# Multiplying the expert one-hots by their gates on ScalarE instead of VectorE

## The reference, cut to what matters

```python
def peer_ffn(h, wq, subkeys, u_tab, v_tab):
    ...
    eidx = jnp.take_along_axis(cidx, pos, axis=-1)    # i1 * 128 + i2
    gate = jax.nn.softmax(best, axis=-1).astype(h.dtype)
    ...
    def expert_block(args):
        hx, ex, gx = args
        act = jax.nn.gelu(jnp.einsum('td,tkd->tk', hx, u_tab[ex]))
        return jnp.einsum('tk,tkd->td', act * gx, v_tab[ex])
```

## Time and profile before

| | us |
|---|---|
| median of 3 runs | 3662.87 |
| lowest and highest | 3655.67, 3663.2 |
| span of the profiled execution | 3655.0 |

### The profile page before, as it was taken

One profiled execution on the slowest core, in us unless ns is written; L12 is line 12 of the kernel. 1 busy time (PEld: TensorE's weight loads), 2 busy tenths in 40 slices (PEclk: granted clock), 3 DMA queues, 4 the chain that ended last, 5 costly groups with the idle time before them and its releaser, 6 DMA issues. The chain is left out here.

```text
span 3655.0 us, 46514 instructions
## 1 busy us (share of the span) xinstructions
PE 3308.5 (91%) x18811; PEld 2594.7 (71%) x18811; DVE 2606.1 (71%) x3318; ACT 1266.7 (35%) x1467; POOL 414.2 (11%) x393
## 2 busy tenths in 40 slices
PE   7989878989889998999999979898999998999898
PEld 5756646788889998778777768666874674543676
DVE  5856768889999997678788854746446444894664
ACT  3323233334445554444444343312322111100333
POOL 0011101100121221133232100011000110000000
PEclk8889889999999999999999989999999999999899
DMA  9974367847989999899999765223645215442663
GB/s 358 379 274 139 115 224 285 314 167 251 330 322 353 363 362 362 322 371 382 369 376 379 274 205 195 80 76 108 216 162 190 67 31 147 138 154 94 220 222 150
DMA packets 294613, 870.30 MB, mean 238 GB/s; under 512 B 33584, under 2 KB 108436, under 8 KB 242432
## 3 DMA queue, kind: packets, MB, share of 16 engines
q1 hardware_dynamic: 257616, 670.64, 51.7%
q0 software_dynamic: 34320, 190.40, 13.6%
q10 hardware_dynamic: 2464, 6.29, 0.5%
HBM read 820.22 MB, written 46.38 MB: 237 GB/s over the span
## 5 line engine op out<-in xcount | busy, mean ns | idle before, releaser
L2489 DVE TENSOR_TENSOR expert_w_low<-expert_w,expert_w_high 128x2048 fp32r<-128x2048 f32 x256 | 585.5, 2287 | 151.1 <-ACT expert_w_high L2916 148.7
L2824 PE MATMUL bank<-h_halves,expert_w_high 128*128 128x384 f32 x2048 | 610.4, 369 | 61.7 <-DVE expert_w_low L2489 61.5
L2916 ACT ACTIVATE expert_w_high<-expert_w 128x2048 fp32r<-128x2048 f32 x256 | 490.4, 1916 | 443.7 <-DMA expert_w<-in_peer_v_dram 298.8
L294 DVE TENSOR_TENSOR weights_low<-weights,weights_high 128x1024 fp32r<-128x1024 f32 (+4 forms) x288 | 338.2, 1177 | 297.4 <-ACT weights_high L277 294.0
L2825 PE MATMUL bank<-h_halves,expert_w_low 128*128 128x192 f32 x2048 | 519.7, 254 | 0.0
L277 ACT ACTIVATE weights_high<-weights 128x1024 fp32r<-128x1024 f32 (+4 forms) x288 | 293.6, 1022 | 468.3 <-PE bank L322 385.2
L2824 PEld LDWEIGHTS bank<-h_halves,expert_w_high 128*128 128x128 f32 x2048 | 393.3, 192 | 72.5 <-DVE expert_w_low L2489 72.1
L2825 PEld LDWEIGHTS bank<-h_halves,expert_w_low 128*128 128x128 f32 x2048 | 399.6, 195 | 0.0
L2893 PE MATMUL bank<-expert_w_high,gated_acts_halves 128*128 128x512 f32 x512 | 203.0, 396 | 22.4 <-DVE expert_w_low L2489 22.1
L2895 PE MATMUL bank<-expert_w_high,gated_acts_halves 128*128 128x512 f32 x512 | 201.0, 393 | 0.0
L2894 PE MATMUL bank<-expert_w_low,gated_acts_halves 128*128 128x512 f32 x512 | 200.9, 392 | 0.0
(11 more groups left out here) (741 smaller groups left out, 6460.5 us busy)
## 6 DMA issues: line engine op xcount, KB each, us to landing
expert_w<-in_peer_u_dram SPq DMA_DIRECT2D x128, 1024.0 KB
expert_w<-in_peer_v_dram SPq DMA_DIRECT2D x128, 1024.0 KB
weights<-in_ada_w_dram SPq DMA_DIRECT2D x88, 512.0 KB, 9.2
weights<-in_w_out_dram SPq DMA_DIRECT2D x32, 1024.0 KB, 13.3
weights<-in_w_in_dram SPq DMA_DIRECT2D x32, 960.0 KB, 8.7
weights<-in_w_in_dram SPq DMA_DIRECT2D x32, 928.0 KB, 9.8
weights<-in_w_in_dram SPq DMA_DIRECT2D x56, 512.0 KB, 7.3
s_gates_w<-in_w_in_dram SPq DMA_DIRECT2D x56, 512.0 KB, 3.5
```

The lines of the kernel that those rows point to most:

```text
L294: dve.tensor_tensor(self.low[:, u % self.UNITS_HELD, :, 0:n], self.buf[b][:, k:k + self.UNIT, 0:n], self.high[:, u % self.UNITS_HELD, :, 0 ...
L2489: dve.tensor_tensor(wl[:, n % RING, :], w_sb[:, n % RING, :], wh[:, n % RING, :], ALU.subtract).then_inc(wl_ready, 1)
L2824: pe.matmul(o[:, 0:2 * DENSE], uh[:, b, k, :], acts.both[:, k, :, 0:DENSE], start=(k == 0), stop=False)
L2916: act.activation(wh[:, n % RING, :], w_sb[:, n % RING, :], ACT.Copy).then_inc(wh_ready, 1)
```

## The change

The in-place multiplication of `hot1` leaves VectorE's program, and with it the two waits of VectorE for itself; the one-hot now signals `first_onehots_ready`. In ScalarE's program the first tile of each group gets, behind `high` and the gelu, a wait for that signal and eight activations of the kind Copy, one for each token, in place on 128 columns, with the token's column of `gateT` as the scale of each partition. The last of them signals `first_onehots_gated`, for which TensorE now waits, beside `hot_ready`, ahead of the gates products of the group. What is computed stays the same.

```diff
--- before.py
+++ after.py
@@ -2473,6 +2473,7 @@
         sk_loaded, turned = m.sem("subkeys_loaded"), m.sem("peer_q_turned")
         shifted, expd, ready, turned_picks = m.sem("best_shifted"), m.sem("best_exp"), m.sem("picks_ready"), m.sem("picks_turned")
         hot_ready, hot_used = m.sem("onehots_ready"), m.sem("onehots_used")
+        first_hot_ready, first_hot_gated = m.sem("first_onehots_ready"), m.sem("first_onehots_gated")
         gates_ready, gates_stored = m.sem("block_gates_ready"), m.sem("block_gates_stored")
         score_ring = BankRing(m.banks[4:8], m.sem("score_banks_filled"), m.sem("score_banks_emptied"))
         h_ring = BankRing(m.banks[0:4], m.sem("own_h_banks_filled"), m.sem("own_h_banks_emptied"))
@@ -2640,9 +2641,8 @@
                     if half == 0:
                         if g >= 2:
                             dve.wait_ge(hot_used, g - 1)
-                        V(dve.tensor_tensor(hot1[:, b, :, :], view(st.iota_row[:, 0:1], [[0, TOK], [1, P]]),
-                                            spread(i1T[:, tok], P), ALU.is_equal))
-                        V(dve.tensor_tensor(hot1[:, b, :, :], hot1[:, b, :, :], spread(gateT[:, tok], P), ALU.mult))
+                        dve.tensor_tensor(hot1[:, b, :, :], view(st.iota_row[:, 0:1], [[0, TOK], [1, P]]),
+                                          spread(i1T[:, tok], P), ALU.is_equal).then_inc(first_hot_ready, 1)
                     else:
                         dve.tensor_tensor(hot2[:, b, :, :], view(st.iota_row[:, 0:1], [[0, TOK], [1, P]]),
                                           spread(i2T[:, tok], P), ALU.is_equal).then_inc(hot_ready, 1)
@@ -2864,6 +2864,7 @@
                         if g == 0:
                             m.to_dve.take_all(pe)
                         pe.wait_ge(hot_ready, g + 1)
+                        pe.wait_ge(first_hot_gated, g + 1)
                         for half in range(2):
                             bank = gates_ring.take(pe)
                             for e in range(TOK // 2):
@@ -2945,6 +2946,13 @@
                         if n == plan.shifted[i] - 2:
                             act.wait_ge(shifted, i + 1)
                             act.activation(best[:, tt, :, :], best[:, tt, :, :], ACT.Exp).then_inc(expd, 1)
+                    g = group_after(n + 1)
+                    if g is not None:
+                        act.wait_ge(first_hot_ready, g + 1)
+                        for t in range(TOK):
+                            hot = hot1[:, g % 2, t, :]
+                            ins = act.activation(hot, hot, ACT.Copy, scale=gateT[:, g * TOK + t:g * TOK + t + 1])
+                        ins.then_inc(first_hot_gated, 1)
                     g = group_after(n)
                     if g is not None:
                         i, place = divmod(g, PER_BLOCK)
```

## The result

The changed kernel is slower: its time is 1.0094 times that of the kernel before, with a 95% interval of 1.0066 to 1.0122 (the two medians of the same comparison, 3701.93 and 3663.03 us, stand at 1.0106). On 3663 us that is +34 us, where +14 was forecast. 3702 us lies above the range of 3651 to 3692. Of each kernel four runs were timed; the profiled run of the kernel before is the fastest of its four, so the two profiled spans differ by more than these 34 us.

What follows compares the result with a forecast made beforehand. VectorE, busy 278.3 of the stage's 282 us, was taken as the bound, with TensorE and DMA close. -16.6 + 5.6 + 25 = +14 us on the 3662.87 us median gave 3677 us; range 3651 to 3692.

Steps and rivals of the forecast that it cites:

- (1): TensorE's period per group in the stage: relieved of the product, VectorE no longer bounds it, 11.76 to 11.07 us, -16.6 us.
- (2): Gelu groups without a store: copies behind ScalarE's gelu make the gates products 0.8 us late, seven times, 5.6 us.
- (3): Five gelu groups after a store: late expert_w loads delay ScalarE's copies, TensorE stands 5.0 us each, 25 us.
- (4): First three groups of the stage: the prediction had no term for waits there, so nothing was added.
- much slower: Rival: scaled copies on ScalarE don't overlap or each pays more than 387 ns, 3.1 us a group; 3693 us, chance 0.10.
- static 6.3: Mean TensorE stop behind a store, from placing 2.43 us of copies behind ScalarE's gelu in the kernel before: 6.3 us.
- keeps its distance to TensorE: Store on SP's queue follows the gates products by 5.1 us; the first load queued behind it doesn't land earlier.
- faster: Rival: VectorE alone is the bound, loads go out earlier and the wait on the copies is met; 3651 us, chance 0.18.
- no difference: Rival: bytes pace the stage, VectorE's freed time becomes waiting for `high`, stops 2.4 us each; 3664 us, chance 0.27.

Runs made afterwards that it cites:

- The later store: Changed kernel with the full 2 MB store of a block of gates moved behind the next load in SP's list: 1.0025, 3675.19 us.
- the small store: Changed kernel with each store of gates cut to 16 of its 128 columns of experts, same place in SP's list: 0.9972, 3657.56 us.

## Why the prediction missed

The sign was right, and so was the place of the loss: gates products that wait for copies that stand behind a late load. The size was not. By the steps of the sum, in the profiled execution, with 24 periods from group to group:

| step | forecast, us | measured, us |
|---|---|---|
| (1) period of a clean group, 11.76 before | 11.07: -16.6 | 11.16: 24 x -0.60 = -14.4 |
| (2) gelu ahead of the copies | 7 x 0.8 = 5.6 | 6 x 0.73 = 4.4 |
| (3) groups behind a store | 5 x 5.0 = 25 | 5 x 7.1 = 35.6 |
| (4) first three groups | nothing | 8.9 |
| others | nothing | 1.3 |
| stage | +14 | +36 |

**The copies** last 390 ns and eight take 2.44 us, against 387 and 2.43 in the forecast. The rival "much slower" falls with its reason, copies that don't overlap, though the measured 3702 lies nearer to its 3693 than to 3677. VectorE's busy time in the stage fell by 22.9 us where some 30 were named; over the whole span it fell by 29.8. TensorE's idle time moved to the gates products, as named. In a group without gelu the gates products wait 0.22 us and, with a gelu, 0.95: step (2) was right to 0.1 us, and so was the choice to let the non-gelu groups pay nothing.

**The step that failed in size is (3)**, the price of a stop behind a store. It has two parts. First, the stop itself was 4.7, 7.8, 4.9, 7.3 and 4.2 us, 5.8 in the mean, where I took 5.0 from a static 6.3. I lowered it because the second load "can go earlier". In three of the five it did: its `high` began 17.2 to 17.9 us behind the store, against 19.2 to 20.8 in the kernel before, and these stops are the 4.2 to 4.9. In the other two the first load alone took 16 us to land, the second `high` began 20.4 and 20.8 us behind the store, and the stops are 7.3 and 7.8. Why two of five are so late stays open. What I had written of the first load came true in all five: the store "keeps its distance to TensorE", and the load is queued behind it, though its buffer is now free 5 us before. From the fifth tile of the stage on, `low` ends 6.5 to 11.7 us before TensorE starts on the tile, instead of 0.1 to 4.4. Second, the gates products behind the stop ran at the lower clock and took 3.1 to 3.4 us instead of 1.78, some 1.5 us more in each, a cost that the sum had no term for. With the 0.2 us that a clean group waits too taken off, 5.8 + 1.5 - 0.2 gives the 7.1 that were measured. The later store and the small store show that the loss hangs on the store's bytes and its place in SP's list together.

**Step (4) was missing.** The first three groups took 14.4, 15.7 and 12.3 us. VectorE's lead was still 0.1 to 2.7 us in the first four tiles, so the tiles were loaded late, and ScalarE's wait for them stood ahead of the copies without any store. The wait of the second group, 2.99 us of idle time, comes from a load issued at 1088.42, with no store near it:

```profile
1097.50 1.92 ACT L2917 ACTIVATE expert_w_high<-expert_w 128x2048 fp32r<-128x2048 f32 x1 [2.09 <-DMA expert_w<-in_peer_u_dram]
1099.32 0.83 ACT L2929 ACTIVATE expert_act<-expert_act 128x768 f32<-128x768 f32 x1
1100.06 2.43 ACT L2954 ACTIVATE query_area<-query_area,gate_cols 128x128 f32<-128x128 f32 x8
```

The lower clock behind this wait, from 1101.6 to 1108.4, slowed the group's products and the start of the third. I looked only for stores, and I priced no clock. The 10.6 us missing in (3) and the 8.9 of (4) carry the time out of the range. That this part has no other cause was not tried by itself; with the copies at the head of the loop these three groups took 11.9, 11.6 and 10.9 us.

**Step (1) came out almost as forecast, and yet it is not a gain of the edit.** "VectorE costs TensorE about 0.69 us in a group" was read as VectorE being the bound. The kernel without the product gains 2.5 us of it; most of the rest goes to the groups behind the stores, which were priced for the copies but not for the evictions and the `low`s that wait there as well. So the rival "faster" was wrong even with free copies, and "no difference", that the bytes pace the stage, describes what a relief of VectorE alone gives. My sum added a gain and a loss that are not independent.

The Trainium skill's rule that multiplications belong on VectorE, in "ScalarE: Activation LUTs", section "Rules for kernel authors", gave +25 by engine time. The trace agrees that VectorE is the faster of the two for this product (1.22 us a group against 2.44), and the sign came out that way, but the difference in engine time is not what was paid: 58.5 us more ScalarE time beside VectorE's product gave 0.9998, and the product on ScalarE gave 0.9999 at one place in its program and 1.0094 at another.

## What to carry to other kernels

Before an engine is relieved, take its work away without a substitute: if that alone gains nothing, a second bound stands close behind, and moving the work has little to gain. On an engine that works in order, work that the critical engine waits for belongs ahead of any wait for a DMA; here its place counted for more than its length. A faster engine frees buffers earlier; look at what stands ahead of the loads in the issuing queue, because a store that waits there holds all of them.

## What the runs showed of the hardware

A stop of TensorE costs more than its length. The stretch behind the stop of 7.8 us (7.60 idle in the timeline), and the one after it, by windows:

```profile
1207.40:1214.20 6.80, 3.79 (x17) 3.82 (x18) 6.80 (x8) 5.99 (x12) 1.89 (x2) 0.50 0.87 292
1214.20:1262.00 47.80, 42.47 (x304) 41.63 (x303) 37.93 (x33) 32.76 (x55) 8.17 (x5) 1.00 0.91 344
```

The granted clock is 0.50, the lower of the two levels (1.2 of 2.4 GHz), in a stretch that begins within the stop (TensorE had run dry at 1202.8) and reaches over the 16 gates products, 3.4 us at this level against 1.78 at the other; then it is 1.00 up to the next stop. The changed kernel has six such stretches in the stage, 34.0 us in all, one at each of the five stores and one at the wait of the second group; the kernel before has three, 10.2 us in all. The length of the stop is not the whole of it: with the later store the products behind a stop of 3.6 us took 1.78 us, and those behind one of 3.4 us took 2.7. In the kernel before the three stretches followed waits of only 1.7 to 1.9 us ahead of the scores, and their groups took 14.4 to 14.6 us; two groups with waits of 1.8 and 1.9 us that the clock did not follow took 13.0.

A 1 MB load issued right behind the 2 MB store came late by more than the hold. In the changed kernel the first load behind each of the five stores landed 9.7 to 16.2 us after its issue (the one issued at 1184.95 at 1201.16) and the second 14.7 to 18.2; the 48 loads of the stage took 8.1 us in the median. With the small stores in the same kernel it was 5.8 to 7.5 and 9.8 to 13.2 us.
